# Layer norms of a hybrid decoder step: sums over eight tiles as a tree of three additions

## The chip, the cores and the metric

The kernel runs on one core of a Trainium2 chip. The metric is the device time of one execution in microseconds, as the median of the runs taken. A profiled execution lists every instruction of the engines: TensorE (PE; its weight loads are listed apart as PEld), VectorE (DVE), ScalarE (ACT), GpSimd (POOL) and the queue of SyncE (SP), which issues the transfers.

## The reference

One decoder layer is computed for a prompt of 2048 tokens and 32 sample tokens (8 sequences of 4), 2080 tokens in all, with 1024 features, in float32. After a token mixer (mLSTM heads and sliding-window attention) and after a SwiGLU of width 2816 stands a layer norm:

```python
def layer_norm(x, g, b):
    xf = x.astype(jnp.float32)
    mu = jnp.mean(xf, -1, keepdims=True)
    var = jnp.mean(jnp.square(xf - mu), -1, keepdims=True)
    return ((xf - mu) * lax.rsqrt(var + LN_EPS) * g + b).astype(x.dtype)
...
x = layer_norm(ALPHA * x + mix @ w_out, ln1_g, ln1_b)
gate, up = jnp.split(x @ w_ffn_in, 2, axis=-1)
x = layer_norm(ALPHA * x + (jax.nn.silu(gate) * up) @ w_ffn_out, ln2_g, ln2_b)
```

The sums that the change touches are those of `mu` and `var`: over the 1024 features of every token.

## The kernel before

**Layout.** The activations lie with features on the partitions: 1024 features are 8 tiles of 128 partitions (KD = 8), and the tokens lie along the free axis. The 2080 tokens are 5 groups of 416 (NG = 5, TG = 416). A group of one activation is a tile of 128 x 8 x 416. Its sum over features has therefore two steps: on VectorE over the eight tiles, which leaves 128 x 416 in the tile `total`, and on PE over the partitions, by a matmul with a matrix whose entries are 1/1024 (`take_mean`, `take_variance`), which leaves the mean in every partition.

**The products.** All large products are made in three passes: weights and activations are both split into a rounded high part (type fp32r) and a low rest, and PE adds high x high, high x low and low x high into one bank. ScalarE makes the high part of a slab of weights, and GpSimd the low part, by a subtraction of the high part from the raw slab (L262 in the projections, L1971 in the later stages). So each step of PE needs one rounding on ScalarE and one subtraction on GpSimd before it.

**Stages.** First the projections and mixers (until about 830 us of the span), then the tail (sample tokens, `tail`, L1250), in which the output product of the last group is made, then `layer` (L1644). Its vector program runs: 44 steps of the first feed-forward product for group 0 (2 x 22 slabs of 128 x 1024 columns; the rows `gated`, L2268 to L2278, are VectorE's part); 16 half steps of the second product; then for two pairs of groups (1, 2) and (3, 4) the first product in seven block products per unit of 22 (`pair_steps`, a scheme with block sums `sum_blocks`, `last_sum`, `hidden`) and 32 half steps of the second product. The order of the work on each engine is written out by hand in those loops.

**The norms** (class `Norm`) lie inside these loops. There are nine numbered ones, 0 to 8, and a last one with a code of its own at the end:
- Norm 0 (the first norm of group 0) in `tail`; `norm_at` gives the slab at which each operation stands.
- Norms 1 to 4 (the first norm of groups 1 to 4) in the 44 steps of `layer`: norm k begins at step 4 + 9 (k - 1), and its operations stand at fixed steps behind that (L1650: sum at 0, mean at 2, sum of squares at 4, variance at 6).
- Norms 5 and 6 (the second norm of groups 0 and 1) in the block products of the two pairs, in parts (L1772): the sums in four parts of 104 tokens each, one part at a product P5 and one at a product P1 of a unit.
- Norms 7 and 8 (the second norm of groups 2 and 3) in the last half steps (`LATE`, L1769).
- The second norm of group 4 behind the last product (L2463 to L2490).

Each norm has a chain over three engines: sum on VectorE, mean on PE, centring on VectorE, square on ScalarE, sum of squares on VectorE, variance on PE, root on ScalarE, reciprocal and scaling on VectorE, gain on ScalarE. PE takes the mean or the variance in program order between two of its steps, so it stands still where the sum isn't done yet. `Norm.reduce` (L1166 to L1170) is the sum over the tiles:

```python
ts = slice(TG // of * part, TG // of * (part + 1))
ins = self.nc.vector.tensor_reduce(self.total[:, ts], self.over_tiles(x[:, :, ts]), AX.X, ALU.add)
```

It is one operation which reads, for each token, the eight values that lie 416 columns apart. The table `NORM` (L1787) names for each norm its tile `x` and a second tile of the same size, `sq`, into which ScalarE writes the squares.

Of the kernel before, what the change touches and what calls it, by code (L numbers as in the profile page):

```python
# [9 lines left out]
ALU = mybir.AluOpType  # L10
ACT = mybir.ActivationFunctionType
AX = mybir.AxisListType
# [3 lines left out]
KD = D // P  # L16
# [47 lines left out]
class Steps:  # L64
# [3 lines left out]
    def __init__(self, eng, sem, turn=0, each=0):  # L68
        self.eng, self.sem, self.turn, self.each, self.k = eng, sem, turn, each, 0
# [1072 lines left out]
class Norm:  # L1142
# [7 lines left out]
    def __init__(self, nc, m, keep, mean, var):  # L1150
        self.nc, self.keep, self.mean, self.var = nc, keep, mean[:, 0:TG], var[:, 0:TG]
        self.total, self.root = m.sb("total", [P, TG]), m.sb("root", [P, TG])
        (self.summed, self.mean_full, self.centred, self.squared, self.sq_summed, self.var_full, self.root_done, self.rstd_done,
         self.scaled, self.ready) = (m.sem("n_" + n) for n in self.SIGNALS)

# [7 lines left out]

    def reduce(self, x, part, of, signal):  # L1166
        ts = slice(TG // of * part, TG // of * (part + 1))
        ins = self.nc.vector.tensor_reduce(self.total[:, ts], self.over_tiles(x[:, :, ts]), AX.X, ALU.add)  # L1168
        if part == of - 1:
            ins.then_inc(signal, 1)  # L1170

    def sum(self, x, part=0, of=1):
        self.reduce(x, part, of, self.summed)

    def sum_squares(self, dve, n, sq, part=0, of=1):
        dve.wait_ge(self.squared, n + 1)
        self.reduce(sq, part, of, self.sq_summed)

    def with_all(self, x, stat, op, part, of, signal):
        ks = slice(KD // of * part, KD // of * (part + 1))  # L1180
# [69 lines left out]
def tail(nc, io, keep, s_inp, outs, stream, chunks, taken, ahead, norm, ps):  # L1250

    cols, ident, sbias = keep["cols"], keep["ident"], keep["sbias"]
    x, L = stream, ahead["S"]
    nxt, ah, al = ahead["nxt"], ahead["ah"], ahead["al"]
# [4 lines left out]
    m = taken["rest"]  # L1259
# [21 lines left out]
    squares = Store(nc, AHEAD_AT).sb("t_squares", [P, KD, TG])  # L1281
# [194 lines left out]
    def vector(dve):  # L1476
        v = Steps(dve, S["v_done"])

        for n in range(CUT, SLABS):
# [72 lines left out]
                nc.vector.tensor_tensor(mix[:, 0:4], wi[:, 0:P].rearrange("p (h t) -> p h t", t=NS), gate[:], ALU.mult).then_inc(sig["mixed"], 1)  # L1552
            if n == norm_at["sum"]:
                dve.wait_ge(L["x_in"], 16)
                norm.sum(nxt[:])
            if n == norm_at["centre"]:
                norm.centre(dve, 0, nxt[:])
            if n == norm_at["sum_sq"]:
# [10 lines left out]
            for b in range(DB):  # L1569
                if UPDATES + b // 2 == n:  # L1570
# [7 lines left out]
                    else:  # L1578
                        v(last)
                        nc.vector.tensor_copy(n0[:].unsqueeze(2), state[:, :, P:P + 1]).then_inc(sig["state"], 1)  # L1580

    return (sync, gpsimd, tensor, scalar, vector), sig["state"]


# [54 lines left out]
def evacuated(r, t):  # L1639

    return (IN if r == 0 else IN + KD + (r - 1) * 2 * KD) + t + 1


def layer(nc, io, keep, stream, ahead, norm, chunk_outs, updated, ps):  # L1644
# [9 lines left out]
    raw4, wlo4, whi3, nxt, raw_in, S = (ahead[n] for n in ("raw", "wlo", "whi", "nxt", "raw_in", "S"))  # L1654

    def memory(name, at, shape):

        return Store(nc, at).sb(name, shape), Store(nc, at).sb(name + "_r", shape, F32R)
# [3 lines left out]
    def low(a, b, rounded=False):  # L1662

        lo, _, t = next(x for x in lows if x[0] <= a < x[1])
        return t[rounded][:, a - lo:b - lo]
# [5 lines left out]
    half = {n: memory("half_" + n, at, [P, HALF, P]) for n, at in (  # L1671
        ("R0", R0), ("R1", R1), ("S", SUMS), ("H", H), ("T", T), ("E0", E0), ("E1", E1), ("E2", E2))}
# [10 lines left out]
    m = Store(nc, 0)  # L1683
# [80 lines left out]
    def norm_steps(n):  # L1764

        return [(k, n - first_norm(k)) for k in range(1, NG) if 0 <= n - first_norm(k) <= STORE]
# [34 lines left out]
    part, mean_sq, mean_copy = (low(i, i + 1)[:, 0] for i in (52, 53, 54))  # L1801
# [465 lines left out]
    def vector(dve):  # L2267
# [87 lines left out]
        def norms(n):  # L2355
            for k, at in norm_steps(n):
                x, sq, which, _, there = NORM[k]
                if at == SUM:
                    dve.wait_ge(S["x_in"], 16 * there)
                    norm.sum(x)  # L2360
                if at == CENTRE:
                    norm.centre(dve, k, x)
                if at == SUM_SQ:
                    norm.sum_squares(dve, k, sq)
                if at == SCALE:
                    norm.invert(dve, k)
                    norm.scale(dve, k, x)

        def pair_norms(r, name, part, of):
            k = 4 + r  # L2370
            x, sq, which, _, there = NORM[k]
            if name == "sum":
                dve.wait_ge(S["x_in"], 16 * there)
                norm.sum(x, part, of)
            if name == "centre":
                norm.centre(dve, k, x, part, of)
            if name == "sum_sq":
                norm.sum_squares(dve, k, sq, part, of)
            if name == "invert":
                norm.invert(dve, k, part, of)  # L2380
            if name == "scale":
                norm.scale(dve, k, x, part, of)

        def late_norms(i):
            k, at = LATE.get(i, (None, None))
            if k is None:
                return
            x, sq, which, _, there = NORM[k]
            if at == "sum":
                dve.wait_ge(S["x_in"], 16 * there)  # L2390
                norm.sum(x)
            if at == "mean":
                norm.centre(dve, k, x)
            if at == "sum_sq":
                norm.sum_squares(dve, k, sq)
            if at == "scale":
                norm.invert(dve, k)
                norm.scale(dve, k, x)
# [30 lines left out]
        def halves(r, n):  # L2429
            for i in range(n):  # L2430
                if i % 2 and not (r == 2 and i == n - 1):
                    add(r, i // 2)
                if r < 2 and i == n - 2:
                    sum_blocks(r + 1, 0)
                    last_sum(r + 1, 0)
                if r and 2 <= i < 2 + len(H_PIECES):
                    a, b = H_PIECES[i - 2]
                    area = AREAS[r][1]
                    dve.wait_ge(S["h_hi"], KF + len(H_PIECES) * (r - 1) + i - 1)
                    nc.vector.tensor_tensor(h_lo(area, a, b), h_lo(area, a, b, False), h_hi(area, a, b).bitcast(F32),  # L2440
                                            ALU.subtract).then_inc(S["h_split"], 1)
                if r < 2:
                    tokens(r + 1, i - X_AT_HALF[r + 1])
                if r == 2:
                    late_norms(i)

        memory_free(dve)
        for n in range(IN):
            if n % 2:
                gated(n // 2)  # L2450
            norms(n)
        halves(0, HALVES)
        for r in (1, 2):
            for n, j, name in pair_steps():
                hidden(r, j, name)
                if name == "P6" and j + 1 < KF:
                    sum_blocks(r, j + 1)
                if name == "P7" and j + 1 < KF:
                    last_sum(r, j + 1)
                pair_norms(r, *pair_part(j, name))  # L2460
            halves(r, 2 * HALVES)

        x = last_x  # L2463
        dve.wait_ge(S["evac"], evacuated(2, 2 * KD - 2))
        norm.sum(x[:, 0:KD - 1])
        dve.wait_ge(norm.mean_full, NORMS + 1)
        move(0, 4)
        move(4, 7)
# [187 lines left out]
```

## Time and profile before

| | |
|---|---|
| median of 3 runs | 2400.22 us (2399.38 to 2400.95) |
| the profiled execution | 2400.25 us, span 2398.5 us |
| PE busy | 2360.5 us, 98% of the span |
| VectorE busy | 1315.3 us, 55% |
| ScalarE busy | 1001.0 us, 42% |
| GpSimd busy | 1251.2 us, 52% |
| granted clock of PE, mean | 0.993 |

How to read it: the span runs from the first to the last instruction, and the execution's own time is 1.75 us longer. A share of busy time is a mean over stages with different limits. A row of the timeline tells start, duration, engine, line, operation, output <- inputs and, in brackets, the idle time before it with what ended it; an instruction that is held up after its issue shows this as a longer duration, not as idle time.

### The profile page before, as it was taken

Reading aid. Unit: us, or ns where it says so; the run is one execution under the profiler, and the core shown is the slowest. Engines: PE = TensorE matmul, PEld = TensorE weight load, DVE = VectorE, ACT = ScalarE, POOL = GpSimd, SP = SyncE. Lnnn points to the kernel's source line nnn. Section 1 sums busy time; section 2 is a strip of 40 time slices with the busy share of each in tenths; the row PEclk is TensorE's granted clock in tenths of the full one; section 3 lists DMA queues with packets and bytes.
Section 4 is the critical chain, followed back from the end, with each engine's and each line's share of the span. In section 5 each row is a group of like instructions: output and inputs, shape, how many; then the busy total and the mean of one; then the engine's idle time right before and its main releaser. Section 6 shows DMA issues by size and latency. Waiting matters only on the chain.

```text
span 2398.5 us, 33775 instructions
## 1 busy us (share of the span) xinstructions
PE 2360.5 (98%) x12923; PEld 2268.6 (95%) x12923; DVE 1315.3 (55%) x2034; ACT 1001.0 (42%) x1673; POOL 1251.2 (52%) x680
## 2 busy tenths in 40 slices
PE   8999999999999999999999999999999999999997
PEld 7999999999999889899999999999999999999997
DVE  4355564555656564677365765554074675554165
ACT  3335554555555433355343444333243444333243
POOL 4455445444454435455465555555465555555543
PEclk9999999999999989999999999999999999999999
DMA  5444434434356765655543223226543222226453
GB/s 197 151 117 137 144 106 140 109 106 135 114 176 195 235 213 172 207 199 171 211 154 115 82 76 105 82 88 221 197 157 133 81 77 96 90 74 237 157 190 109
DMA packets 147492, 345.31 MB, mean 144 GB/s; under 512 B 14366, under 2 KB 93302, under 8 KB 145142
## 3 DMA queue, kind: packets, MB, share of 16 engines
q1 hardware_dynamic: 147334, 343.17, 44.4%
q8 instruction: 103, 1.69, 0.3%
q14 instruction: 55, 0.45, 0.1%
HBM read 290.30 MB, written 53.84 MB: 143 GB/s over the span
## 4 chain that ended last, share of the span: by engine, by line
PE 90%; DVE 4%; DMA 3%; issue 1%; ACT 1%; SPq 0%; ACTq 0%; DVEq 0%
PE acc L275 9%; PE acc L2170 9%; PE acc L277 9%; PE acc L2171 9%; PE acc L2174 9%; PE acc L276 9%; PE fb L2170 5%; PE fb L2171 5%; PE fb L2174 5%; PE kd L2170 4%; PE kd L2171 4%; PE kd L2174 4%; DVE total L1168 2%; PE fb L630 1%; PE w L607 1%
## 5 line engine op out<-in xcount | busy, mean ns | idle before, releaser
L262 POOL TENSOR_TENSOR wlo<-raw,whi 128x1024 fp32r<-128x1024 f32 x150 | 370.7, 2475 | 464.2 <-ACT whi L256 464.1
L275 PE MATMUL acc<-xh,whi 128*128 128x416 f32 x1200 | 433.5, 361 | 0.0
L277 PE MATMUL acc<-xh,wlo 128*128 128x416 f32 x1200 | 425.6, 355 | 0.0
L276 PE MATMUL acc<-xl,whi 128*128 128x416 f32 x1200 | 422.5, 352 | 0.0
L1971 POOL TENSOR_TENSOR l_wlo<-l_raw,blocks_hi 128x512 fp32r<-128x512 f32 x176 | 226.7, 1299 | 200.3 <-DVE l_raw L2297 150.9
L256 ACT ACTIVATE whi<-raw 128x1024 fp32r<-128x1024 f32 x150 | 158.6, 1057 | 402.8 <-PE acc L277 295.4
L275 PEld LDWEIGHTS acc<-xh,whi 128*128 128x128 f32 x1200 | 227.9, 190 | 8.4 <-issue 6.3
L1971 POOL TENSOR_TENSOR sums_r<-sums,blocks_hi 128x512 fp32r<-128x512 f32 x132 | 170.7, 1294 | 115.7 <-ACT blocks_hi L2033 89.4
L276 PEld LDWEIGHTS acc<-xl,whi 128*128 128x128 f32 x1200 | 228.0, 190 | 3.1 <-issue 0.2
L277 PEld LDWEIGHTS acc<-xh,wlo 128*128 128x128 f32 x1200 | 227.3, 189 | 2.9
L2170 PE MATMUL acc<-low_r,blocks_hi 128*128 128x416 f32 x608 | 216.9, 357 | 0.0
L894 DVE COPY ring<-acc 128x416 f32<-128x416 f32 (+4 forms) x154 | 66.7, 457 | 195.0 <-PE acc L277 194.8
L1971 POOL TENSOR_TENSOR l_wlo<-l_raw,l_whi 128x1024 fp32r<-128x1024 f32 x41 | 103.9, 2537 | 99.9 <-ACT l_whi L2120 99.9
L2033 ACT ACTIVATE blocks_hi<-l_raw 128x512 fp32r<-128x512 f32 x176 | 109.9, 626 | 97.0 <-PE acc L2174 48.7
L289 DVE TENSOR_TENSOR xl<-xraw,xh 128x832 fp32r<-128x832 f32 x52 | 112.1, 2172 | 55.4 <-ACT xh L250 55.4
L2057 ACT ACTIVATE temps<-temps 128x416 f32<-128x416 f32 x88 | 48.6, 552 | 193.6 <-DVE temps L2317 133.8
L1971 POOL TENSOR_TENSOR half_R_r<-half_R,half_H_r 128x1408 fp32r<-128x1408 f32 x24 | 80.3, 3346 | 84.3 <-ACT half_H_r L2019 84.3
L2171 PE MATMUL acc<-low_r,blocks_hi 128*128 128x416 f32 x348 | 122.9, 353 | 0.0
L1971 POOL TENSOR_TENSOR half_R_r<-half_R,half_T_r 128x1408 fp32r<-128x1408 f32 x25 | 88.6, 3544 | 63.4 <-ACT half_T_r L2019 63.2
L2170 PEld LDWEIGHTS acc<-low_r,blocks_hi 128*128 128x128 f32 x608 | 114.5, 188 | 3.2 <-issue 0.3
L2170 PE MATMUL kd<-low_r,blocks_hi 128*128 128x416 f32 x312 | 111.5, 357 | 0.0
L2170 PE MATMUL fb<-low_r,blocks_hi 128*128 128x416 f32 x312 | 110.9, 355 | 0.0
(509 smaller groups left out, 5734.0 us busy)
## 6 DMA issues: line engine op xcount, KB each, us to landing
l_raw<-in_wB SPq DMA_DIRECT2D x132, 512.0 KB, 3.6
raw<-in_wA SPq DMA_DIRECT2D x110, 512.0 KB, 3.6
half_R<-in_w SPq DMA_DIRECT2D x52, 704.0 KB, 4.3
raw<-in_wB SPq DMA_DIRECT2D x40, 512.0 KB, 4.1
half_S<-in_w SPq DMA_DIRECT2D x25, 704.0 KB, 4.3
xraw<-in_xT SPq DMA_DIRECT2D x32, 416.0 KB, 5.4
hb<-temps SPq DMA_DIRECT2D x44, 208.0 KB, 1.9
stage<-in_xT SPq DMA_DIRECT2D x40, 208.0 KB, 4.0
```

The lines of the kernel that those rows point to most:

```text
L256: self.nc.scalar.activation(self.whi[:, n % 3], self.raw[:, n % 4], ACT.Copy).then_inc(self.hi_done, 1)
L262: self.nc.gpsimd.tensor_tensor(self.wlo[:, n % 4], self.raw[:, n % 4], self.whi[:, n % 3].bitcast(F32), ALU.subtract).then_inc(self.lo_don ...
L275: pe.matmul(bank[:, 0:TG], hi[:, a], self.xh[x][:, a], start=(a == 0), stop=False)
L276: pe.matmul(bank[:, 0:TG], hi[:, a], self.xl[x][:, a], start=False, stop=False)
L277: last = pe.matmul(bank[:, 0:TG], lo[:, a], self.xh[x][:, a], start=False, stop=(a == KD - 1))
L289: self.nc.vector.tensor_tensor(self.xl[x][:, ks], self.xraw[x][:, ks], self.xh[x][:, ks].bitcast(F32), ALU.subtract).then_inc(self.x_split, 1)
L894: last = nc.vector.tensor_copy(dst, acc[k % 2][:, col:col + size])
L1971: nc.gpsimd.tensor_tensor(lo, raw, hi.bitcast(F32), ALU.subtract).then_inc(S["lo_done"], 1)
L2033: nc.scalar.activation(blocks_hi[:, n % 4], weights(r, j, name, False), ACT.Copy).then_inc(S["hi_done"], 1)
L2170: pe.matmul(to, hi[:, c], xh, start=(first and c == 0), stop=False)
L2171: pe.matmul(to, hi[:, c], xl, start=False, stop=False)
L2174: ins = pe.matmul(to, lo[:, c], xh, start=False, stop=(last and c == len(xs) - 1))
```

## The change

`reduce` makes the sum over eight tiles by three additions: four tiles plus four, two plus two, one plus one. The first writes into a tile `to`, the second works in place there, and the third writes `total`. Behind each of the first two VectorE waits until it is complete (a new semaphore, `halves`). For the sum of x, `to` is the norm's tile for the squares, which is written so earlier than before; for the sum of squares it is the tile of squares itself. Norms 0 to 8 use it, in the same places as before. The last norm's sum over seven tiles stays one operation, now written out in `layer`.

```diff
-    def reduce(self, x, part, of, signal):
+    def reduce(self, dve, x, to, part, of, signal):
+
         ts = slice(TG // of * part, TG // of * (part + 1))
-        ins = self.nc.vector.tensor_reduce(self.total[:, ts], self.over_tiles(x[:, :, ts]), AX.X, ALU.add)
+        for half in (4, 2):
+            a = x if half == 4 else to
+            self.halved += 1
+            self.nc.vector.tensor_tensor(to[:, 0:half, ts], a[:, 0:half, ts], a[:, half:2 * half, ts], ALU.add).then_inc(self.halves, 1)
+            dve.wait_ge(self.halves, self.halved)
+        ins = self.nc.vector.tensor_tensor(self.total[:, ts], to[:, 0, ts], to[:, 1, ts], ALU.add)
         if part == of - 1:
             ins.then_inc(signal, 1)

-    def sum(self, x, part=0, of=1):
-        self.reduce(x, part, of, self.summed)
+    def sum(self, dve, x, room, part=0, of=1):
+
+        self.reduce(dve, x, room, part, of, self.summed)

     def sum_squares(self, dve, n, sq, part=0, of=1):
         dve.wait_ge(self.squared, n + 1)
-        self.reduce(sq, part, of, self.sq_summed)
+        self.reduce(dve, sq, sq, part, of, self.sq_summed)
...
-                norm.sum(nxt[:])
+                norm.sum(dve, nxt[:], squares[:])
...
-                    norm.sum(x)
+                    norm.sum(dve, x, sq)
...
-                norm.sum(x, part, of)
+                norm.sum(dve, x, sq, part, of)
...
-        norm.sum(x[:, 0:KD - 1])
+        nc.vector.tensor_reduce(norm.total[:], norm.over_tiles(x[:, 0:KD - 1]), AX.X, ALU.add).then_inc(norm.summed, 1)
```

VectorE's order at norm 1, in the first feed-forward product of group 0, before (`low_184` is the norm's tile, `low_186` that of the squares; `temps` and `low_r` belong to `gated`):

```order
L2273 TENSOR_TENSOR temps<-temps,acc 128x416
L2276 CAST low_r<-temps 128x416
L2278 TENSOR_TENSOR low_r<-temps,low_r 128x416
L1168 TENSOR_REDUCE total<-low_184 128x416
L2273 TENSOR_TENSOR temps<-temps,fb 128x416
L2276 CAST low_r<-temps 128x416
L2278 TENSOR_TENSOR low_r<-temps,low_r 128x416
L1181 TENSOR_TENSOR low_184<-low_184,w 128x3328
L2273 TENSOR_TENSOR temps<-temps,acc 128x416
L2276 CAST low_r<-temps 128x416
```

and now (the new operation is on L1174 and L1176, and the lines behind it are nine further down):

```order
L2282 TENSOR_TENSOR temps<-temps,acc 128x416
L2285 CAST low_r<-temps 128x416
L2287 TENSOR_TENSOR low_r<-temps,low_r 128x416
L1174 TENSOR_TENSOR low_186<-low_184 128x1664
L1174 TENSOR_TENSOR low_186<-low_186 128x832
L1176 TENSOR_TENSOR total<-low_186 128x416
L2282 TENSOR_TENSOR temps<-temps,fb 128x416
L2285 CAST low_r<-temps 128x416
L2287 TENSOR_TENSOR low_r<-temps,low_r 128x416
L1190 TENSOR_TENSOR low_184<-low_184,w 128x3328
L2282 TENSOR_TENSOR temps<-temps,acc 128x416
L2285 CAST low_r<-temps 128x416
```

Each reduction has become three additions in the same place; nothing else on VectorE, and nothing on the other engines, has changed its order.

VectorE's order at two parts of norm 5 in a unit of the first pair's block products, before (L2337 to L2341 are the combinations of P4 and P3, the reductions stand at P1 and P5):

```order
L2337 TENSOR_TENSOR low_r<-temps,low_r 128x416
L1168 TENSOR_REDUCE total<-low_182 128x104
L2339 TENSOR_TENSOR temps<-temps,acc 128x416
L2341 TENSOR_TENSOR temps<-temps 128x416
L1168 TENSOR_REDUCE total<-low_182 128x104
```

and now:

```order
L2346 TENSOR_TENSOR low_r<-temps,low_r 128x416
L1174 TENSOR_TENSOR low_182<-low_182 128x4x104
L1174 TENSOR_TENSOR low_182<-low_182 128x2x104
L1176 TENSOR_TENSOR total<-low_182 128x104
L2348 TENSOR_TENSOR temps<-temps,acc 128x416
L2350 TENSOR_TENSOR temps<-temps 128x416
L1174 TENSOR_TENSOR low_182<-low_182 128x4x104
L1174 TENSOR_TENSOR low_182<-low_182 128x2x104
L1176 TENSOR_TENSOR total<-low_182 128x104
```

Three additions of 4 x 104, 2 x 104 and 104 columns stand in the place of a reduction to 104.

## Rows read from the trace of the kernel before

**Rows 1.** The page, part 1: busy time, share of span, instructions of each engine.
```profile
PE 2360.5 (98%) x12923; PEld 2268.6 (95%) x12923; DVE 1315.3 (55%) x2034; ACT 1001.0 (42%) x1673; POOL 1251.2 (52%) x680
```

**Rows 2.** Timeline, weight loads of the norms' matmuls: start, us, engine, line, [idle before <-releaser].
```profile
988.97 0.30 PEld L1204 LDWEIGHTS w<-total,mean_of 128*128 128x128 f32 x2 [2.52 <-DVE total L1168]
...
1030.95 0.38 PEld L1204 LDWEIGHTS w<-total,mean_of 128*128 128x128 f32 x2
...
1049.73 0.38 PEld L1208 LDWEIGHTS w<-total,mean_of 128*128 128x128 f32 x2
...
2293.56 0.30 PEld L1204 LDWEIGHTS w<-total,mean_of 128*128 128x128 f32 x2 [1.00 <-DVE total L1168]
...
2328.27 0.30 PEld L1204 LDWEIGHTS w<-total,mean_of 128*128 128x128 f32 x2 [1.10 <-DVE total L1168]
...
2342.33 0.30 PEld L1208 LDWEIGHTS w<-total,mean_of 128*128 128x128 f32 x2 [0.90 <-DVE total L1168]
```

**Rows 3.** Groups by line and form, VectorE, the reductions: busy us, mean ns.
```profile
L1168 DVE TENSOR_REDUCE total<-low 128x416 f32<-128x3328 f32 x9 | 57.3, 6371 | 5.3 <-ACT low L1215 5.3
...
L1168 DVE TENSOR_REDUCE total<-low 128x104 f32<-128x832 f32 x12 | 20.6, 1718 | 2.9 <-PE acc L2174 2.5 <-PE kd L2174 0.4
```

**Rows 4.** Groups by line and form, VectorE, additions of two SBUF tiles.
```profile
L2426 DVE TENSOR_TENSOR low<-low 128x416 f32<-128x416 f32 x2 | 1.2, 593 | 0.1
...
L2426 DVE TENSOR_TENSOR low<-low 128x832 f32<-128x832 f32 x1 | 1.0, 1025 | 0.3 <-ACT low L2155 0.3
```

**Rows 5.** Timeline at 1738 to 1752 us, VectorE, then GpSimd.
```profile
1738.81 1.89 DVE L2406 TENSOR_TENSOR low<-low,low 128x1664 f32<-128x1664 f32 x1 [8.13 <-DMA low<-x]
1740.74 1.89 DVE L2408 TENSOR_TENSOR low<-low 128x1664 f32<-128x1664 f32 x1
1742.55 4.93 DVE L2410 TENSOR_TENSOR low<-low 128x1664 f32<-128x1664 f32 x1
...
1741.98 3.74 POOL L1971 TENSOR_TENSOR half_R_r<-half_R,half_H_r 128x1408 fp32r<-128x1408 f32 x1 [7.13 <-ACT half_H_r L2019]
1745.69 4.88 POOL L1971 TENSOR_TENSOR half_S_r<-half_S,half_T_r 128x1408 fp32r<-128x1408 f32 x1
```

**Rows 6.** Timeline at 977 to 990 us (sum of norm 1), VectorE, then GpSimd.
```profile
980.10 2.68 DVE L2278 TENSOR_TENSOR low_r<-temps,low_r 128x416 fp32r<-128x416 f32 x1
...
977.42 9.99 POOL L1971 TENSOR_TENSOR l_wlo<-l_raw,l_whi 128x1024 fp32r<-128x1024 f32 x4 [2.93 <-ACT l_whi L2120]
988.01 2.37 POOL L1971 TENSOR_TENSOR l_wlo<-l_raw,l_whi 128x1024 fp32r<-128x1024 f32 x1 [0.60 <-ACT l_whi L2120]
```

**Rows 7.** Timeline at 1024 to 1049 us (both sums of norm 2), VectorE, then GpSimd.
```profile
1024.01 6.43 DVE L1168 TENSOR_REDUCE total<-low 128x416 f32<-128x3328 f32 x1
...
1042.79 6.39 DVE L1168 TENSOR_REDUCE total<-low 128x416 f32<-128x3328 f32 x1
...
1025.07 2.44 POOL L1971 TENSOR_TENSOR l_wlo<-l_raw,l_whi 128x1024 fp32r<-128x1024 f32 x1 [3.67 <-ACT l_whi L2120]
1028.53 2.40 POOL L1971 TENSOR_TENSOR l_wlo<-l_raw,l_whi 128x1024 fp32r<-128x1024 f32 x1 [1.02 <-ACT l_whi L2120]
...
1042.28 2.86 POOL L1971 TENSOR_TENSOR l_wlo<-l_raw,l_whi 128x1024 fp32r<-128x1024 f32 x1 [2.10 <-ACT l_whi L2120]
1046.80 2.42 POOL L1971 TENSOR_TENSOR l_wlo<-l_raw,l_whi 128x1024 fp32r<-128x1024 f32 x1 [1.66 <-ACT l_whi L2120]
```

**Rows 8.** Timeline at 2287 to 2330 us (norms 7 and 8), VectorE, then GpSimd.
```profile
2287.22 6.29 DVE L1168 TENSOR_REDUCE total<-high 128x416 f32<-128x3328 f32 x1
...
2288.24 3.25 POOL L1971 TENSOR_TENSOR half_R_r<-half_R,half_T_r 128x1408 fp32r<-128x1408 f32 x1 [3.04 <-ACT half_T_r L2019]
...
2328.46 3.23 POOL L1971 TENSOR_TENSOR half_S_r<-half_S,half_H_r 128x1408 fp32r<-128x1408 f32 x1 [8.64 <-ACT half_H_r L2019]
```

**Rows 9.** Timeline at 1305 to 1312 us (a unit of norm 5's parts), GpSimd, then PE.
```profile
1305.94 1.29 POOL L1971 TENSOR_TENSOR l_wlo<-l_raw,blocks_hi 128x512 fp32r<-128x512 f32 x1 [3.41 <-DVE l_raw L2297]
...
1310.91 0.92 PE L2174 MATMUL kd<-low_r,l_wlo 128*128 128x416 f32 x4
```

More of the change, by code:

```diff
@@ L1152, in __init__ @@
         self.total, self.root = m.sb("total", [P, TG]), m.sb("root", [P, TG])
+        self.halves, self.halved = m.sem("n_halves"), 0
         (self.summed, self.mean_full, self.centred, self.squared, self.sq_summed, self.var_full, self.root_done, self.rstd_done,
@@ L2390, in late_norms @@
                 dve.wait_ge(S["x_in"], 16 * there)
-                norm.sum(x)
+                norm.sum(dve, x, sq)
             if at == "mean":
```

## The prediction

> **What bounds the kernel now.** I read the page first: TensorE (PE) is busy for 98% of the span [rows 1], so only what makes PE wait, or stop waiting, changes the time. Next I listed, on PE's weight loads, the waits in front of the two matmuls of each norm (L1204 takes the mean, L1208 the variance). Five loads stand idle for VectorE's reduction (DVE, L1168): 2.52 us at the mean of norm 1, and near the end 1.00 us twice in norm 7, 1.10 and 0.90 us in norm 8, 6.52 us together [rows 2] (one of the two loads of norm 7 stands there). The loads at 1030.95 (mean of norm 2) and 1049.73 (its variance) wait for nothing: there PE arrives after the reduction is done. So a quicker reduction can give at most 6.52 us, and a slower one costs PE time wherever it ends after PE arrives.
>
> **What is removed and added.** 30 reductions go: 14 over a whole group of 416 tokens (norms 0 to 4, 7 and 8, two each) and 16 over 104 tokens (norms 5 and 6, four parts for each of two sums). A whole one takes 6.37 us and a part 1.72 us [rows 3]. The last reduction, over seven tiles, stays as it is. Each one that goes is replaced by three additions, of 1664, 832 and 416 columns (416, 208 and 104 in a part), the second and third behind a wait on the one before.
>
> Undisturbed, an addition with both inputs in SBUF takes 1.89 us for 1664 columns [rows 5], 1.03 for 832 and 0.59 for 416 [rows 4]. Between two that wait on each other lie 0.04 us (L2406 ends at 1740.70, L2408 starts at 1740.74 [rows 5]), so a whole tree takes 1.89 + 1.03 + 0.59 + 0.08 = 3.59 us: 2.8 us less than the reduction.
>
> **What the disturbance costs.** GpSimd (POOL) makes the low parts of the weights all through these stages, by one subtraction of two SBUF tiles per step. [Rows 5] show such additions and subtractions shutting each other out. L2408 ends at 1742.63; POOL's subtraction, ready at 1741.98, ends at 1745.72, 3.09 us later. L2410, issued at 1742.55, takes 4.93 us in place of 1.89 and ends at 1747.48, 1.76 us after POOL's end. POOL's next, issued at 1745.69, takes 4.88 and ends 3.09 us after that. They take turns: whoever ends lets in the other that waits. A reduction is not held up: the one at 1024.01 runs with POOL busy beside it for most of its time and takes 6.43 us, near the mean of all [rows 3, 7]. The Trainium skill has this rule ("SBUF — State Buffer", section "Who interferes with whom"): two SBUF inputs on VectorE contend with a GpSimd instruction that reads SBUF, one is fully blocked by the other, and a reduce never contends. It speaks against this change and the rows agree with it.
>
> So each tree offers POOL two openings between its additions. After a release I price the blocked addition at 1.75, 0.87 and 0.43 us (its columns at the pace of the 1.76 us above), a POOL step of 1024 columns at 2.27 us (1042.28 + 2.86 = 1045.14, less the end of the addition before it at 1042.87, where the reduction's row starts at 1042.79 with the usual overlap [rows 7]), and one of 1408 columns at 3.09 us.
>
> *Norm 1, sum.* VectorE comes out of a subtraction that was itself blocked (2.68 us, to 982.78). POOL works off four steps in a row until 987.41, and a fifth comes at 988.01 [rows 6]. The third of the four has the turn; it ends at 987.41 - 2.42 = 984.99. Addition 1 ends at 986.74, POOL's fourth at 989.01, addition 2 at 989.88, POOL's fifth at 992.15, addition 3 at 992.58. PE's wait ended at 988.97 [rows 2]; it would end at 992.6: **+3.65 us**. Lower bound: had the burst of POOL not been there, the tree would end at 986.4 and give back the 2.5 us.
>
> *Norm 2, sum* [rows 7]. Addition 1 runs from 1024.01 to 1025.90; POOL, ready at 1025.07, runs to 1028.17; addition 2 to 1029.04; POOL, ready at 1028.53, to 1031.31; addition 3 to 1031.74. PE asks at 1030.95: **+0.85 us** with the hand-over.
>
> *Norm 2, squares* [rows 7]. At 1042.87 POOL has the turn until 1045.14; addition 1 ends at 1046.89; POOL, ready at 1046.80, runs to 1049.16; addition 2 ends at 1050.03; POOL has nothing then, addition 3 ends at 1050.66. PE asks at 1049.73: **+1.0 us**.
>
> *Norm 4* starts, as norm 2 does, at an odd step behind a gate's evacuation, with POOL in the same place: again **+1.85 us**. Norm 3 starts at an even step, a step of PE earlier against PE's question, and the second sum of norm 1 meets one POOL step: both end before PE asks and cost nothing. So does norm 0: POOL's steps there are a whole slab of PE apart, and with one let in a tree takes 3.59 + 2.27 = 5.86 us, less than the reduction.
>
> *Norms 7 and 8* [rows 8]. In three of the four sums a POOL step of 1408 columns becomes ready about 1 us after the start. For the first: addition 1 from 2287.26 to 2289.15, POOL to 2292.24, addition 2 to 2293.11, addition 3 to 2293.74, against 2293.51 for the reduction: +0.2 us, three times. For the sum of norm 8 POOL stands idle for 8.64 us up to 2328.46, the tree is clean, and PE's 1.10 us [rows 2] goes. Together 0.6 - 1.1 = **-0.5 us**.
>
> *Norms 5 and 6.* A part's tree takes about 0.59 + 0.37 + 0.27 + 0.08 = 1.3 us clean (the two small ones estimated from the slope of [rows 4]); every POOL step of 512 columns let in adds up to 1.29 [rows 9], so typically 2.6 to 3.9 us against 1.72. What waits behind it are VectorE's combinations and block sums of the next unit, then POOL's low part. The cover: that low part is ready at 1307.23 and PE uses it at 1310.91, 3.7 us later [rows 9]. I count zero; without the cover it is a rival below.
>
> POOL is held up by at most 1.9 us at a time in the norms; its steps run ahead of PE by about a step (4.5 us between POOL's rows in [rows 7]), so this costs nothing.
>
> **Sum:** 3.65 + 0.85 + 1.0 + 1.85 - 0.5 = 6.85 us. The profiled execution took 2400.25 us (span 2398.5), the median of the runs is 2400.22, so no correction: **2407 us**, 0.29% slower. About 0.2%, 4.8 us, is what a measurement of this kernel can tell from no change.
>
> A second place in the Trainium skill points the other way: "VectorE: DVE Perf Modes", section "The perf-mode tier table", gives the reduce the same one element per cycle as a float32 tensor_tensor. By that the reduction of 3328 columns would take about 3.5 us, an estimate from the page, the tree would have nothing to win even when clean, and the sum would be 1.1 us higher, 8 us. The rows say 6.37 against 3.59 us [rows 3 to 5], and I go by them.
>
> **The rivals.**
>
> *A. The additions run clean, or keep their turn through the tree: faster or no change.* Deciding point: VectorE's next addition is in before POOL's waiting step. Clean, every tree takes 3.59 us, all five waits go: -6.5 us, 2393.7. If only the first addition waits for a POOL step under way and the other two follow at once, norm 1 ends at 986.74 + 1.7 = 988.4 (-0.5), norms 2 and 4 end before PE asks, norms 7 and 8 lose their 4.0 us of waits: -4.5, 2395.7. For it: the 0.04 us between two additions is short. Against it: the exact alternation in [rows 5]. Chance 0.15, of which 0.1 is faster by over 0.2%. The skill's VectorE page, section "Rules for kernel authors", advises to restructure a tensor_reduce on a hot path; that would be this case.
>
> *B. Norm 1 costs little.* The 3.65 us rest on a backlog of POOL's from late weight loads. If the tree starts where the backlog has ended, one POOL step falls into it, it ends about level with the reduction, and the sum is 3.2 us: 2403.4, within 0.2%. For it: loads vary between runs. Against it: the blocked row at 980.10 shows the backlog is set by POOL's own pace. Chance 0.17.
>
> *C. The parts of norms 5 and 6 break their cover: slower still.* Two parts that follow each other in one unit can add up to 2 x 2.2 = 4.4 us, over the 3.7 us, so 0.7 us of waiting in each of six such units: +4, 2411. For it: each small tree takes three turns. Against it: not all three will meet POOL. Chance 0.13.
>
> **How the numbers follow.** Forecast 0.55 (2404 to 2409.5), A 0.15, B 0.17, C 0.13. The range 2400 to 2411.5 leaves out A and part of C. Slower by over 0.2% (above 2405.0): C and nearly all of the forecast, 0.64. Faster (below 2395.4): 0.1. Within: the rest of A, B and the forecast's low edge, 0.26.
>
> **What would show it.** Right: L1174 rows of 1664 columns lasting 2.7 to 4.2 us in norms 1, 2 and 4; between two additions of a tree a POOL row; PE's wait at norm 1's mean near 6 us and new waits of about 1 us at norms 2 and 4; none at the sum of norm 8. Wrong: additions at 1.89, 1.03 and 0.59 us throughout and no wait of PE at L1204 or its like.

## The result, and the profile after

The change takes 2410.62 us (median of four runs, 2408.44 to 2412.58); beside it the kernel before took 2399.8. The ratio is 1.0044, 95% interval [1.0033, 1.0056]: slower by 8 to 13 us. The forecast was 2407 us, the range 2400 to 2411.5. The sign, the mechanism and most places were right; the size was 3.6 us too small, in the main for two terms that the prediction had at nothing.

Part 1 of the page of the change, the profiled execution of 2408.44 us (span 2406.7):

```profile
PE 2361.5 (98%) x12923; PEld 2266.9 (94%) x12923; DVE 1355.6 (56%) x2094; ACT 1000.5 (42%) x1673; POOL 1268.1 (53%) x680
```

PE does the same work [rows 1]. VectorE is 40 us longer busy with 60 instructions more, though a clean tree is shorter than a reduction: its additions are being held up. GpSimd is 17 us longer busy with the same 680 instructions: so are its subtractions.

The timeline of the change, PE's weight loads at the norms (L1213 takes the mean, L1217 the variance; in the brackets PE's wait):

```profile
989.84 0.50 PEld L1213 LDWEIGHTS w<-total,mean_of 128*128 128x128 f32 x2 [6.12 <-DVE total L1176]
...
1034.97 0.30 PEld L1213 LDWEIGHTS w<-total,mean_of 128*128 128x128 f32 x2 [0.86 <-DVE total L1176]
...
1054.71 0.30 PEld L1217 LDWEIGHTS w<-total,mean_of 128*128 128x128 f32 x2 [1.03 <-DVE total L1176]
...
1120.87 0.30 PEld L1213 LDWEIGHTS w<-total,mean_of 128*128 128x128 f32 x2 [0.87 <-DVE total L1176]
...
1140.62 0.30 PEld L1217 LDWEIGHTS w<-total,mean_of 128*128 128x128 f32 x2 [1.03 <-DVE total L1176]
...
1324.02 0.30 PEld L1213 LDWEIGHTS w<-total,mean_of 128*128 128x128 f32 x2 [0.84 <-DVE total L1176]
...
1879.34 0.30 PEld L1213 LDWEIGHTS w<-total,mean_of 128*128 128x128 f32 x2 [0.57 <-DVE total L1176]
...
2302.43 0.30 PEld L1213 LDWEIGHTS w<-total,mean_of 128*128 128x128 f32 x2 [1.20 <-DVE total L1176]
...
2316.78 0.30 PEld L1217 LDWEIGHTS w<-total,mean_of 128*128 128x128 f32 x2 [1.20 <-DVE total L1176]
...
2337.54 0.19 PEld L2179 LDWEIGHTS acc<-low_r,half_H_r 128*128 128x128 f32 x1 [0.95 <-DVE low L2362]
...
2350.52 0.30 PEld L1217 LDWEIGHTS w<-total,mean_of 128*128 128x128 f32 x2 [0.52 <-DVE total L1176]
```

Against [rows 2], place by place, in us:

| place | predicted | wait before | wait after | difference |
|---|---|---|---|---|
| norm 1, mean | +3.65 | 2.52 | 6.12 | +3.60 |
| norm 2, mean and variance | +0.85, +1.0 | none | 0.86, 1.03 | +1.89 |
| norm 4, mean and variance | +1.85 | none | 0.87, 1.03 | +1.90 |
| norms 5 and 6, mean | 0 | none | 0.84, 0.57 | +1.41 |
| norm 7, mean and variance | +0.4 | 1.00, 1.00 | 1.20, 1.20 | +0.40 |
| norm 8, mean and variance | -0.9 | 1.10, 0.90 | 0.95, 0.52 | -0.53 |

At norms 0 and 3 and at the variance of norm 1 no load waits, as predicted. The waits sum to +8.7 us. The rest is not a wait. The norm 1 load starts at 988.97 before and 989.84 after, the next such load, at the mean of norm 2, at 1030.95 and 1034.97: 41.98 us against 45.13. Of the 3.15 us more, 0.86 are the wait at norm 2, and **2.3 us** remain. The stretches in a windows query (busy time and instructions of PE, PEld, VectorE, ScalarE, GpSimd, then the granted clock, DMA share and GB/s), of the kernel before:

```profile
990.00:1000.00 10.00, 10.00 (x55) 9.91 (x54) 9.90 (x7) 4.87 (x3) 2.81 (x2) 1.00 0.20 56
```

and of the change:

```profile
990.00:1000.00 10.00, 10.00 (x40) 9.07 (x41) 6.43 (x7) 2.31 (x2) 1.17 (x1) 0.77 0.13 35
```

PE is called busy for all of 990 to 1000 in both, but does 55 products before and 40 after. The granted clock is 0.77 in place of 1.00. Here are two products of that stretch in the timeline of the change:

```profile
993.82 0.55 PE L2180 MATMUL acc<-xl,l_whi 128*128 128x416 f32 x1
...
997.62 0.35 PE L2180 MATMUL kd<-xl,l_whi 128*128 128x416 f32 x1
```

The same form takes 0.55 us, and 0.35 from 994.8 on. Behind the long wait PE runs at the lower of its two levels (1.2 GHz; the granted clock from 990 to 994 us is 0.50), later at the higher (2.4 GHz; 1.00 from 995 us on). 8.7 + 2.3 = 11.0 us, and the medians of the three sets of the change lie 10.8, 10.4 and 9.8 us above the kernel before. The two profiled executions differ by 8.2 us only, since PE put its question for norm 1 at 989.84 - 6.12 = 983.72 in this one and at 988.97 - 2.52 = 986.45 before. That is ahead of the first norm in `layer`, and two more profiles of the change have it at 985.38 and 986.94. The granted clock from 840 to 940 us goes with it: 0.93, 0.91 and 0.90 in these three, 0.90 in the kernel before. Two kernels with the reduction in all norms up to there have 0.90 and 0.95 (experiments 4 and 3), so I take this spread as one between executions, not of the change.

How the sum of norm 1 came to be late: VectorE of the change, then GpSimd:

```profile
979.97 7.17 DVE L1174 TENSOR_TENSOR low<-low 128x1664 f32<-128x1664 f32 x2
987.17 2.61 DVE L1176 TENSOR_TENSOR total<-low 128x416 f32<-128x416 f32 x1
...
974.69 14.64 POOL L1980 TENSOR_TENSOR l_wlo<-l_raw,l_whi 128x1024 fp32r<-128x1024 f32 x5 [2.90 <-ACT l_whi L2129]
```

Five subtractions of GpSimd follow each other without a gap, and the three additions take 9.81 us among them, 979.97 to 989.78. The prediction had 982.78 to 992.58, which is 9.80. And norm 2, the sum, in the same order:

```profile
1027.17 5.04 DVE L1174 TENSOR_TENSOR low<-low 128x1664 f32<-128x1664 f32 x2
1032.24 2.68 DVE L1176 TENSOR_TENSOR total<-low 128x416 f32<-128x416 f32 x1
...
1028.22 3.10 POOL L1980 TENSOR_TENSOR l_wlo<-l_raw,l_whi 128x1024 fp32r<-128x1024 f32 x1 [3.66 <-ACT l_whi L2129]
1031.68 2.79 POOL L1980 TENSOR_TENSOR l_wlo<-l_raw,l_whi 128x1024 fp32r<-128x1024 f32 x1 [0.36 <-ACT l_whi L2129]
```

The third addition, 0.59 us by itself [rows 4], was issued at 1032.24, behind a subtraction that ran until 1034.47, and ended at 1034.92, 0.45 us later: the turns and the prices of the prediction.

### The profile page after: what moved, and what is told of

Its sections match the earlier page's. It is cut to its first block, busy times and chain, and to the rows that moved or that the text cites. A ratio compares the mean times of both kernels' runs of the same rounds, so it can differ in the third digit from the quotient of the medians.

```text
span 2406.7 us, 33835 instructions
## 1 busy us (share of the span) xinstructions
PE 2361.5 (98%) x12923; PEld 2266.9 (94%) x12923; DVE 1355.6 (56%) x2094; ACT 1000.5 (42%) x1673; POOL 1268.1 (53%) x680
## 4 chain that ended last, share of the span: by engine, by line
PE 86%; DVE 7%; DMA 3%; issue 2%; ACT 1%; SPq 1%; ACTq 0%; DVEq 0%
PE acc L275 9%; PE acc L277 9%; PE acc L276 9%; PE acc L2179 8%; PE acc L2180 8%; PE acc L2183 8%; PE fb L2179 4%; PE fb L2180 4%; PE fb L2183 4%; PE kd L2179 4%; PE kd L2183 4%; PE kd L2180 4%; DVE low L1174 2%; PE fb L630 1%; DMA raw<-in_wB 1%
## 5 line engine op out<-in xcount | busy, mean ns | idle before, releaser
L1980 POOL TENSOR_TENSOR l_wlo<-l_raw,blocks_hi 128x512 fp32r<-128x512 f32 x176 | 232.0, 1329 | 203.4 <-DVE l_raw L2306 146.0
L1980 POOL TENSOR_TENSOR sums_r<-sums,blocks_hi 128x512 fp32r<-128x512 f32 x132 | 176.9, 1343 | 102.3 <-ACT blocks_hi L2042 79.1
```

What stands on the lines that cost most here:

```text
L1980: nc.gpsimd.tensor_tensor(lo, raw, hi.bitcast(F32), ALU.subtract).then_inc(S["lo_done"], 1)
```

## The experiments

The kernels of one set ran on one chip, beside runs of the kernel before, which took 2395.4 to 2404.9 us in the first set (23 runs).

**1. The change again** (two runs of it, in the first and the third set; no edit).

> The change once more, unaltered: its four runs lay in two groups, about 2408.6 and 2412.5 us, while those of the kernel before lay within 3 us. Theory 'one price' (the trees meet GpSimd's steps in the same places each time): all runs within 2 us of each other, and the gap was an accident of those runs. Theory 'a turn that falls either way' (some addition and some step of GpSimd become ready within a few tens of ns of each other, so the order between them changes from run to run): two groups about 4 us apart again. The median is 2408 to 2413 us by both, 1.0035 to 1.0055 of the kernel before.

> The change unaltered, beside the next run on the same chip. 1.0035 to 1.0055 of the kernel before, as in its nine runs so far; in its profile the granted clock falls to half once between 985 and 1000 us.

Measured: 2409.45 us, 1.0045 [1.0032, 1.0058], and 2409.98 us, 1.0040 [1.0026, 1.0053]. The ten runs lie between 2408.0 and 2412.5. Those of the first set fall into two groups again, 2408.0 to 2409.5 and 2412.2 to 2412.5, so the theory of one price, with all runs within 2 us, missed; those of the third set are less clear (2408.9 to 2410.6, and 2412.3). The kernel before spread more widely over its 23, so such a gap need not come from the trees. The three profiles of the change show the same turns and the same waits of PE, but all three are of runs below 2411 us: what sets the slower ones apart stays open. The clock fell behind norm 1 in both new profiles (0.66 from 990 to 1000 us).

**2. The tree in norm 1 alone, and everywhere but there.** The new function was kept, with a condition in front; the first kernel had `TREE = (1,)`, the second all but 1:

```diff
+        if n not in TREE:
+            ins = self.nc.vector.tensor_reduce(self.total[:, ts], self.over_tiles(x[:, :, ts]), AX.X, ALU.add)
+            if part == of - 1:
+                ins.then_inc(signal, 1)
+            return
```

> The tree in norm 1 alone, the reduction in all other norms. Theory (alternation, place by place): the sum of norm 1 ends 3.6 us later, and nothing else moves: +3.6 us, 1.0015. Rival (the cost is spread over all trees, by more instructions and waits): 2 of the 30 sums give about a fifteenth of the whole, +0.6 us, 1.0003. If the two groups of runs come from norm 1, its runs spread over 4 us.

> The tree in all norms but norm 1. Theory: what is left is norm 2 (+1.9), norm 4 (+1.9), norms 5 and 6 (+1.4), norms 7 and 8 (about 0): +5 us, 1.0021. Rival (spread over all trees): nearly the whole difference stays, +8 us or more, 1.0034. If the two groups of runs do not come from norm 1, they are seen here.

Measured: norm 1 alone 2405.85 us, 1.0026 [1.0015, 1.0037], 6.8 us above the kernel before beside it (2399.01); all but norm 1 2404.37 us, 1.0022 [1.0013, 1.0030], 5.4 us. The rival, a cost spread over all trees, falls: 2 of 30 sums bring more than half. But 6.8 is not the 3.6 of my theory. The timeline of the kernel with norm 1 alone, the loads at the means of norms 1 and 2:

```profile
991.56 0.50 PEld L1221 LDWEIGHTS w<-total,mean_of 128*128 128x128 f32 x2 [6.15 <-DVE total L1184]
...
1036.98 0.30 PEld L1221 LDWEIGHTS w<-total,mean_of 128*128 128x128 f32 x2 [0.78 <-DVE total L1175]
```

and a stretch of its windows query:

```profile
990.00:1000.00 10.00, 8.44 (x29) 7.51 (x30) 6.68 (x6) 0.19 (x1) 1.06 (x1) 0.66 0.01 2
```

The wait is 3.63 us longer; the clock is 0.66, and from 991.56 to 1036.98 pass 45.42 us in place of 41.98. Of these 3.44 us, 0.78 are a wait for norm 2's reduction, which comes late in the wake of norm 1 (PE waited for nothing there before), and 2.66 the clock. 3.63 + 2.66 + 0.78 = 7.1 us. With the tree everywhere else the load of norm 1 waits 2.56 us and the clock stays at 1.00. The time is near the +5 us expected, but one place is not: at the mean of norm 2 PE waits for nothing in this profile. The first two additions there:

```profile
1025.60 2.95 DVE L1182 TENSOR_TENSOR low<-low 128x1664 f32<-128x1664 f32 x2
```

They run clean. GpSimd's subtraction is ready at 1027.83, 2.23 us behind the start of the first (1.05 us in the change, 1028.22 against 1027.17), so only one turn is paid, and the sum ends at 1031.27, before PE asks. How many turns a tree pays can thus hang on a microsecond.

**3. The tree in norms 5 and 6 alone, and in norms 2 and 4 alone** (`TREE = (5, 6)` and `(2, 4)`).

> The tree in the parts of norms 5 and 6 alone. Theory (PE's question for the mean stands right behind the last part): +1.4 us, 1.0006, all of it at the two waits before the means of norms 5 and 6. Rival (the parts break the cover of GpSimd's low parts): up to +4 us, 1.0017, with waits spread over the products of the units. If the two groups of runs come from here, its runs spread over 4 us. My prediction had zero here.

> The tree in norms 2 and 4 alone. Theory (alternation with GpSimd's steps, both sums ending 0.9 and 1.0 us behind PE's question): +3.7 us as predicted, +3.5 by the trace of the change, 1.0015; waits of 0.8 to 1.1 us at four places. Rival (these waits were brought by the delay of norm 1, which shifts VectorE against GpSimd): nothing, 1.0000.

Measured: norms 5 and 6 2400.68 us, 1.0005 [0.9996, 1.0013]. The timeline of this kernel:

```profile
1317.69 0.30 PEld L1221 LDWEIGHTS w<-total,mean_of 128*128 128x128 f32 x2 [0.84 <-DVE total L1184]
...
1872.46 0.30 PEld L1221 LDWEIGHTS w<-total,mean_of 128*128 128x128 f32 x2 [0.54 <-DVE total L1184]
```

1.4 us at the two means, as in the change; the runs (+1.7 us) fit and do not settle it by themselves. Norms 2 and 4: 2402.55 us, 1.0006 [0.9997, 1.0015], 2.4 us more than before. Its profile has the four waits of the change, without any delay at norm 1 (two of the four):

```profile
1029.94 0.30 PEld L1221 LDWEIGHTS w<-total,mean_of 128*128 128x128 f32 x2 [0.87 <-DVE total L1184]
1049.68 0.30 PEld L1225 LDWEIGHTS w<-total,mean_of 128*128 128x128 f32 x2 [1.02 <-DVE total L1184]
```

So the rival of a mere shift behind norm 1 falls by the trace, as the one cause of these waits. At the mean of norm 2 the tree in norm 1 alone is enough too: it brought 0.78 us there behind a reduction (experiment 2). The runs alone, with an interval that holds both zero and 3.6 us, could not have said so.

**4. Norm 1 made late without a tree.** The reductions of before, and in norm 1's sum one more:

```diff
+            if n == 1 and signal is self.summed:
+                self.nc.vector.tensor_reduce(self.root[:, 0:256], self.over_tiles(x[:, :, 0:256]), AX.X, ALU.add)
```

> No tree at all: the reductions of before, and in front of norm 1's sum a second reduction over 256 of the 416 tokens, into a buffer that nobody reads then. It should take 256/416 of 6.4 us, 3.9 us, and so PE's wait at the mean of norm 1 grows from 2.5 to about 6.4 us, as with the tree, without a VectorE instruction that GpSimd can hold up. In the change and in the two kernels with a tree in norm 1, PE's granted clock fell to half right behind that wait; before, and with the tree everywhere but in norm 1, it did not. Theory (the long wait itself brings the half clock): the clock falls here too, behind 990 us, and the kernel loses the wait and 2 to 3.4 us more: +6 to +7.3 us, 1.0025 to 1.0030. Rival (the fall has to do with the tree, or came by chance): the clock stays, +3.9 us, 1.0016.

Measured: 2403.81 us, 1.0018 [1.0008, 1.0027], 4.2 us. By the time alone that is the rival's number. The trace says otherwise, in the loads at the means of norms 1 and 2

```profile
991.41 0.50 PEld L1223 LDWEIGHTS w<-total,mean_of 128*128 128x128 f32 x2 [6.07 <-DVE total L1177]
...
1034.80 0.38 PEld L1223 LDWEIGHTS w<-total,mean_of 128*128 128x128 f32 x2
```

and in a stretch of the windows query:

```profile
990.00:1000.00 10.00, 8.59 (x36) 7.75 (x37) 7.87 (x8) 1.60 (x2) 0.46 (x1) 0.83 0.07 12
```

The wait is 3.55 us longer and the clock does fall, to 0.83, without a single tree. It cost 43.39 - 41.98 = 1.4 us here, less than the 2.3 to 2.8 us in the profiles with the tree in norm 1: 5.0 us by the trace. The direction of the theory held, and its price was too high.

**5. PE kept busy through the wait of norm 1.** The change, and in front of the mean of norm 1 products of a constant with itself:

```diff
     def take_mean(self, pe, n):
+        if n == 1:
+            for _ in range(18):
+                pe.matmul(self.spare[:, 0, 0:P], self.keep["mean_of"][:], self.keep["mean_of"][:], start=True, stop=True)
```

> The change as it is, with 18 small products on PE (128 columns, of a constant with itself, into a bank that nobody uses) in front of its wait for the sum of norm 1. They should take about 18 x 0.27 = 4.9 us, an estimate from the 0.86 us of the two 416-column products of a mean, less than the 6.1 us of the wait. Theory (PE's idleness brings the half clock): the clock stays at its full level behind 990 us, the products there take 0.35 us and not 0.55 to 0.69, and the time falls by 2 to 3.4 us, to 2406 to 2407.5 us, 1.0030 to 1.0036 of the kernel before. Rival (the half clock has to do with anything else, or with the weights that arrive late before 985 us): it falls as before, no change against the change, 1.0045.

> The change with PE kept busy in front of norm 1's mean, once more, beside the change on the same chip, since the two were timed in different sets before (1.0035 and 1.0045, their intervals overlapping) and the profiled run had a late weight near 1162 us. Theory (the half clock is what the idle PE pays for afterwards): no half clock between 985 and 1000 us, 2 to 3.4 us less than the run beside it. Rival (the clock stays, but the time goes elsewhere, since something else would have made PE wait there): no half clock, and within 1 us of the run beside it.

Measured: 2408.38 us, 1.0035 [1.0023, 1.0048] (2406 to 2407.5 expected), and beside the change 2407.98 us, 1.0028 [1.0017, 1.0039], against 2409.98: 2.0 us less, with intervals that overlap. The timeline of the second, the means of norms 1 and 2 and, further on, ScalarE's first rounding of the weights that arrive near 1160 us and PE's first load of them:

```profile
988.50 0.30 PEld L1217 LDWEIGHTS w<-total,mean_of 128*128 128x128 f32 x2 [1.99 <-DVE total L1177]
...
1031.37 0.30 PEld L1217 LDWEIGHTS w<-total,mean_of 128*128 128x128 f32 x2 [0.87 <-DVE total L1177]
...
1165.74 1.38 ACT L2032 ACTIVATE half_E_r<-half_R 128x1408 fp32r<-128x1408 f32 x1 [4.62 <-DMA half_R<-in_w]
...
1167.23 0.29 PEld L2183 LDWEIGHTS kd<-low_r,half_E_r 128*128 128x128 f32 x1 [2.49 <-issue]
```

and the stretch of its windows query:

```profile
990.00:1000.00 10.00, 10.00 (x55) 9.91 (x54) 6.97 (x6) 5.32 (x4) 3.10 (x2) 1.00 0.26 61
```

The same late sum, and the clock stays at 1.00; 55 products again. Between the two loads pass 42.87 us, which is 41.98 and the wait of 0.87, with nothing left over (42.86 in the first run's profile, with a wait of 0.86). So the half clock behind norm 1 is what the idle PE pays afterwards, and it is gone there when PE is not idle.

But by the profiles the rival was right about the time. In both profiles of this kernel the weights near 1160 us are waited for longer, 4.62 and 4.30 us on ScalarE where the change has 3.15 to 3.17. PE's load of them stands for 2.49 us (1.05 in the change beside it), and behind that the clock falls here:

```profile
1165.00:1170.00 5.00, 2.82 (x9) 2.66 (x9) 1.56 (x3) 3.55 (x3) 2.81 (x1) 0.70 0.76 310
```

The change keeps 1.00 there. From the variance of norm 4 to the mean of norm 5 pass 185.09 us against 182.96 in the change beside it: 2.1 us are given back. From the load of norm 1 to the end of the span pass 1415.3 us against 1415.8 in the change beside it; the first profile of this kernel has 1415.3, that of the change in the first set 1416.2. So only 0.5 to 0.9 us are gained behind norm 1, and the 2.0 us of the medians are not shown to come from there.

The transfers of this kernel between the issue of the first of these weights (1156.49) and its rounding (1165.74), 9.25 us, hold one packet that is no data:

```profile
q8 instruction: 1, 0.02, 0.6%
```

It is a fetch of instructions, and the other profile of this kernel has one there too (8.93 us from issue to rounding). The kernel of experiment 6 has one of another queue (8.21 us); in the nine other profiles none falls between the two, and they take 7.77 to 7.81 us. PE's program is 72 instructions longer here ahead of that place, which would bring a fetch forward. That the fetch holds the weights up fits all twelve profiles; no run tests it by itself.

**6. The sum with one side in PSUM.** In the whole norms 1 to 4, 7 and 8; `to` is a pair of banks that `layer` does not use, and each step waits for the one before. Norm 0 and the parts of norms 5 and 6 keep the reduction.

```diff
+            to = self.pair[:, :, 0:TG]
+            steps = [lambda: self.nc.vector.tensor_copy(to, x[:, 0:2]),
+                     lambda: self.nc.vector.tensor_tensor(to, to, x[:, 2:4], ALU.add),
+                     lambda: self.nc.vector.tensor_tensor(to, to, x[:, 4:6], ALU.add),
+                     lambda: self.nc.vector.tensor_tensor(to[:, 1], to[:, 1], x[:, 7], ALU.add),
+                     lambda: self.nc.vector.tensor_tensor(self.total[:], to[:, 0], x[:, 6], ALU.add)]
...
+            ins = self.nc.vector.tensor_tensor(self.total[:], self.total[:], to[:, 1], ALU.add)
```

> In the whole norms 1 to 4, 7 and 8 the sums are made by additions again, but each with one side in PSUM: two tiles are copied there, two additions of two tiles and three of one tile follow; norm 0 and the parts of norms 5 and 6 keep the reduction. Theory (what the tree loses it loses because both inputs of its additions lie in SBUF, against GpSimd's subtraction): none of these steps is held up, each takes what the clean rows show (1.0 us for 832 columns, 0.6 for 416), a sum takes about 5.0 us in place of 6.4, PE's wait at the mean of norm 1 falls from 2.5 to 1.2 us, those of norms 7 and 8 by 1 us each at most, and the new waits at norms 2 and 4 are gone: 3 to 4.5 us faster than before, 0.9981 to 0.9988. Rival (it is the chain of waits between additions, or any long run of VectorE additions, that lets GpSimd in): the steps stretch to 2 to 5 us as in the change, and it is 4 us slower or more, 1.0017 and above.

Measured: 2394.79 us, 0.9981 [0.9972, 0.9990], 4.8 us faster than the kernel before (3 to 4.5 expected) and by the two ratios (0.9981 and 1.0040 to 1.0045) some 15 us faster than the change. The timeline of the sum of norm 1, VectorE, GpSimd, then PE's load there, and the one load of norms 7 and 8 that still waits:

```profile
981.98 1.01 DVE L1176 COPY ce<-low 128x832 f32<-128x832 f32 x1
983.03 1.03 DVE L1177 TENSOR_TENSOR ce<-ce,low 128x832 f32<-128x832 f32 x1
984.10 1.03 DVE L1178 TENSOR_TENSOR ce<-ce,low 128x832 f32<-128x832 f32 x1
985.16 0.60 DVE L1179 TENSOR_TENSOR ce<-ce,low 128x416 f32<-128x416 f32 x1
985.80 0.59 DVE L1180 TENSOR_TENSOR total<-ce,low 128x416 f32<-128x416 f32 x1
986.42 0.59 DVE L1185 TENSOR_TENSOR total<-total,ce 128x416 f32<-128x416 f32 x1
...
976.71 9.97 POOL L1989 TENSOR_TENSOR l_wlo<-l_raw,l_whi 128x1024 fp32r<-128x1024 f32 x4 [2.92 <-ACT l_whi L2138]
...
987.06 0.30 PEld L1222 LDWEIGHTS w<-total,mean_of 128*128 128x128 f32 x2 [1.35 <-DVE total L1185]
...
2324.76 0.19 PEld L2188 LDWEIGHTS acc<-low_r,half_H_r 128*128 128x128 f32 x1 [0.96 <-DVE low L2371]
```

Six steps with five waits between them, in the middle of four subtractions of GpSimd, and not one is stretched: 5.03 us from 981.98 to 987.01. The subtractions take 9.97 us, as in [rows 6]. So neither the waits between additions nor a run of them lets GpSimd in: it is two inputs in SBUF. By place the waits fall by 1.17 us at norm 1, 2.00 at norm 7, and 1.10 - 0.96 + 0.90 = 1.04 at norm 8, 4.2 us together.

The Trainium skill says this too ("SBUF — State Buffer", section "Who interferes with whom"): a VectorE instruction with at most one input in SBUF, outside the modes that use both of its ports, does not contend with GpSimd. The trace agrees, with the 5.03 us above against 9.81 us for the tree in the same place.

## Why the prediction came out as it did

**The bound and the mechanism: right.** The price of a turn (0.43 us behind a release for 416 columns; measured 0.45 at 1034.92), the strict alternation, and GpSimd's backlog at norm 1 gave 3.65, 1.85 and 1.85 us for norms 1, 2 and 4; the waits measure 3.60, 1.89 and 1.90. Rivals A (clean, or the turn kept) and B (norm 1 costs little) fall with the rows of norm 1. At the mean of norm 2 the agreement is partly luck: the tree paid one turn less there in the kernel without a tree in norm 1, and the tree in norm 1 alone brought nearly the same wait, behind a reduction (both in experiment 2).

**The step that failed: norm 1 was priced by its wait alone.** "it would end at 992.6: **+3.65 us**" treats a longer wait of PE as worth its length. The wait brought a stretch at half clock behind it, 2.3 us in this profile and 2.4 to 2.8 in three others with the tree in norm 1 (1.4 with the longer reduction). Experiment 4 shows the fall with no tree at all, experiment 5 its absence at norm 1 with the late sum but a busy PE. This term, missing from the sum, is most of the 3.6 us by which the forecast fell short.

**Norms 5 and 6: "I count zero" was wrong by 1.4 us,** and rival C did not have the place either. The cover that I read was GpSimd's low part (3.7 us, [rows 9]); what runs out is another one, that of the last part in front of PE's mean. Before, the last part's reduction and PE's load at the mean of norm 5:

```profile
1312.47 1.72 DVE L1168 TENSOR_REDUCE total<-low 128x104 f32<-128x832 f32 x1
...
1316.06 0.38 PEld L1204 LDWEIGHTS w<-total,mean_of 128*128 128x128 f32 x2
```

The sum is ready at 1314.19, 1.87 us before it is asked for. The same part in the change:

```profile
1320.61 3.07 DVE L1174 TENSOR_TENSOR low<-low 128x416 f32<-128x416 f32 x2
1323.70 0.27 DVE L1176 TENSOR_TENSOR total<-low 128x104 f32<-128x104 f32 x1
```

It takes 3.36 us in place of 1.72, behind a subtraction of GpSimd that was under way (until 1321.83) and with another let in (until 1323.44); the estimate was 2.6 to 3.9 us. It also starts late: VectorE is 8.14 us behind the kernel before (1320.61 against 1312.47), PE only 7.12 (1324.02 - 0.84 = 1323.18 against 1316.06), which takes 1.02 us of the cover. Together 1.64 + 1.02 = 2.66 us, against 1.87: 0.79 of the 0.84 us of the wait. I asked who waits for GpSimd behind the part, and not who waits for the last part itself.

**Norms 7 and 8: -0.5 predicted, -0.13 measured.** The +0.2 of each of the three sums with a step let in came out. So did the clean tree in norm 8. In the timeline of the change, VectorE, then ScalarE:

```profile
2330.92 1.88 DVE L1174 TENSOR_TENSOR low<-high 128x1664 f32<-128x1664 f32 x1
2332.84 1.03 DVE L1174 TENSOR_TENSOR low<-low 128x832 f32<-128x832 f32 x1
2333.90 0.59 DVE L1176 TENSOR_TENSOR total<-low 128x416 f32<-128x416 f32 x1
...
2331.04 5.12 ACT L1237 ACTIVATE high<-high,gb 128x416 f32<-128x416 f32 x8 [5.50 <-DVE high L1190]
2336.07 1.36 ACT L2028 ACTIVATE half_H_r<-half_S 128x1408 fp32r<-128x1408 f32 x1
```

3.57 us, and PE's wait of 1.10 at the mean is gone. But PE now stands 0.95 us at the first load behind the mean, 2337.54. The profile names a VectorE row there that ended at 2337.19; what ends last is ScalarE's rounding of these very weights, from 2336.07 to 2337.43, behind the eight gains of norm 7. The prediction named the stall that goes, and not what is late next. PE, 0.63 us later for it on balance (0.95 against two short waits of 0.16 before), then waits 0.52 in place of 0.90 at the variance.

**The range.** It held the time (2410.62, under 2411.5) because rival C, an error of the same size and sign, had widened it, not because its mechanism was seen. That is luck.

## What to carry to other kernels

Before a reduction is replaced by additions on VectorE, look at what GpSimd does in the same microseconds: two inputs in SBUF take turns with its subtractions, and a chain of short dependent additions then pays a turn for each. Put one side into PSUM, and additions run at their own pace (0.59 us for 416 columns, 1.03 for 832). And price a new wait of PE at its length plus the clock behind it: look in the profile for what the granted clock did after waits of that length, and count with both outcomes where it did not always do the same.

## What was not expected of the hardware

- A wait of PE of 6.1 us brought half the clock behind it, in each of the profiles with such a wait and an idle PE (1.4 to 2.8 us lost); one of 2.5 us in the same place did not, nor one of 1.99 us behind products that nobody needed. But one of 2.49 us near 1167 us did (0.70, experiment 5), so its length alone does not tell.
- A chain of additions with one side in PSUM costs GpSimd nothing: 9.97 us for four subtractions beside it, and 9.99 beside the reduction [rows 6].
- With PE kept busy at norm 1, weights some 170 us later were waited for 1.1 and 1.5 us longer on ScalarE, in the two profiles of that kernel. A packet of instructions among their transfers goes with it; that it is the cause is not shown.
